# Input projection of a hybrid encoder step: six of seven column groups computed as block pairs with seven products each

## The chip, the cores and the metric

The kernel runs on one NeuronCore of a Trainium2 chip. TensorE (PE) multiplies; VectorE (DVE), ScalarE (ACT) and GpSimd (POOL) do elementwise work; SyncE (SP) issues most DMAs. Each engine runs its own list of instructions strictly in order and waits on semaphores. The metric is the device time of one execution in microseconds. Before the change it is 3000.38 us, the median of three runs (2999.57 to 3002.46).

## The reference, cut to what matters

```
h = rmsnorm(x, norm1_w) * (1 + sc1) + sh1                 # x: 2048 prompt rows, and 32 sample rows
mq, mk, mv, mo, mi, mf, sq, sk, sv = split_proj(h @ p['w_in'])   # 7 groups of 512 columns, 8 gate columns
y_a = rmsnorm(mlstm(mq, mk, mv, mi, mf)) * sigmoid(mo)
q_b, k_rows = rmsnorm(sq per head of 64), rmsnorm(sk per head of 64)
y_b = rmsnorm(stick_breaking(q_b, k_rows, sv))
x = x + g1 * (concat(y_a, y_b) @ p['w_out'])
x = x + g2 * conv_ffn(rmsnorm(x) * (1 + sc2) + sh2)
```

Only `h @ w_in` is touched: 1024 inputs, 7 x 512 + 8 outputs. The sample rows have their own state and modulation but the same weights. In the kernel the groups are numbered 0 mq, 1 mk, 2 mv, 3 sv, 4 mo, 5 sq, 6 sk, and it takes them in the order 0, 1, 2, 3, 5, 6, 4.

## The kernel before, in words

Three phases follow each other, each a block of instruction lists for all five engines with a barrier between: `front` (modulation, first norm, projection, gates), `attention`, and `mlstm_output_ffn`. Only `front` changes, and two scratch tensors in DRAM are added.

Products in fp32 precision are made from three passes in a rounded format: each operand is split into a high part (a rounded copy, by ACT) and a low part (the rest, by DVE or POOL), and high x high, low x high and high x low are summed in PSUM. One tile of 128 tokens by 512 columns by 1024 inputs is so 8 x 3 = 24 matmuls of 512 columns. The sample rows are tile 16; their high and low rows stand beside each other in one tile, so it takes 16 matmuls, and the two partial results are joined afterwards.

`front` has two stretches that matter here.

The prologue is group 0. It also makes `h`. For each of the 17 token tiles: SP loads x (`load_x`, L260); ACT squares and sums it and takes the root (`spread`, L331 and L333); DVE scales it (`scale_rows`, L459); PE transposes it (`turn_x`, L734); ACT and DVE apply scale and shift (`shift`, L352 and L464); ACT rounds it to the high part (L326); POOL makes the low part (`low`, L645); PE multiplies (`project`, L767); ACT moves the result from PSUM to a staging tile (`take`, L368); SP stores it (`store`, L277). There are three x buffers, four PSUM banks for results, and two for transposed x. The order is written out by hand: on ACT, item t is `take(t)`, `shift(t + 2)`, `spread(t + 4)`; on SP, `load_x(t + 3)` stands before `store(t)`, so that `load_x(t + 4)` stands behind `store(t)`; on PE, `project(t)` and then `turn_x(t + 2)`. The eight gate columns follow in one piece (`gates`, L783 and L785).

Groups 1 to 6 then run from SBUF alone: `h` stays there in high and low parts, and the next group's weights come in beneath the running one. In groups 5 and 6 DVE norms each tile per head (L560 to L571), PE transposes it (`turn`, L812), and the high and low parts go to DRAM for the attention (`store_turned`, L672 and L673). Group 4, with no norm, is last.

The later FFN phase already uses products of the new kind: its down projection (L3058) multiplies in units of seven products of 12 matmuls of 512 columns, and its sample rows (`sample_down`, L3029) in plain fp32.

Of the kernel before, what the change touches and what calls it, by code (L numbers as in the profile page):

```python
# [119 lines left out]
def front(k, c, gc, dec, firstK, firstQ):  # L120

    nc, d = k.nc, k.d
    NG, NN = 7, 2
    ORDER = (0, 1, 2, 3, 5, 6, 4)
    G0 = ORDER.index(5)
    FIRST = G0 * NT
    NQ = NG * KD
    NR, NW, NS, NB, NX = 2, 12, 3, 4, 3
    AHEAD = NW - KD
# [3 lines left out]
    END = (NG * NT - 1) % NS  # L133
    spans = [(n * W5, W5) for n in range(SEQ // W5)] + [(SEQ, P)]
    thirds = ((0, 172), (172, 342), (342, W5))

# [8 lines left out]
    raw_in = [k.sem(f"w_raw_loaded{n}") for n in range(2 * NR)]  # L145
    w_low_dve = k.sem("w_low_by_dve")
    w_high, w_low, w_used, summed, taken = k.sems("w_high", "w_low", "w_used", "projected", "psum_taken")
# [5 lines left out]
    sample_copied, sample_joined = k.sems("sample_copied", "sample_joined")  # L153
    wg_high, wg_low, gates_summed, gates_taken, pad_stored = k.sems(
        "wg_high", "wg_low", "gates_summed", "gates_taken", "pad_stored")
    gates_stored = [k.sem(f"gates_stored{n}") for n in range(3)]
# [6 lines left out]
        "rows_stored", "initial_ready", "last_kept", "norm_weights_loaded")  # L163
    with ExitStack() as s:
        with ExitStack() as early:
            h_plain = [sbuf(nc, early, f"h1_plain{n}", [P, KD, TOK]) for n in range(2)]
            xs = sbuf(nc, early, "px", [P, NX + 1, D])
        hH = sbuf(nc, s, "h1H", [P, KD, TOK], F32R)
        hL = sbuf(nc, s, "h1L", [P, KD, TOK], F32R)
        late = sbuf(nc, s, "plate", [P, NW - KD, 2, W5], F32R)  # L170
# [4 lines left out]
        nst = sbuf(nc, s, "pnst", [P, 2, 3, SH])  # L175
        nw = sbuf(nc, s, "pnw", [P, 2, SD])
# [18 lines left out]
        ada = h_plain[1][:, :, 0:4 * W5]  # L195
        bias, rows = h_plain[0][0:2, 0, 0:4 * W5], h_plain[0][0:2, 1, 0:4 * W5]
# [4 lines left out]
        h_raw = lambda t: h_plain[1][:, :, tok(t)]  # L201
        qH = lambda m: turnbuf[:, m % 2].rearrange("p (j e) -> p j e", e=P)
        qL = turnbuf[:, 2].rearrange("p (j e) -> p j e", e=P)
        sq, pT = R[:, 0:2], R[:, 2].rearrange("p (j e) -> p j e", e=P)
        g_out = lambda n, w: turnbuf[0:8, n % 3, 0:w].bitcast(F32)
# [9 lines left out]
        def normed(n):  # L215
            return FIRST <= n < FIRST + NN * NT

# [4 lines left out]
        def raw_slot(q):  # L222

            if q < 2 * KD:
                return q % NR, q // NR
# [3059 lines left out]
```

## Time and profile before

| | us |
|---|---|
| median of 3 runs | 3000.38 |
| the profiled execution | 3003.76 |
| its span, first to last instruction | 3002.1 |
| prologue (first `project` to last gate matmul) | 41.3 to 162.3 |
| groups 1 to 6 | 162.3 to 724.0 |
| first matmul of the attention | 728.3 |
| mean granted TensorE clock | 0.985 |

The span is what lies between the first and the last instruction of the profiled execution; the execution is 1.7 us longer. PE is busy 2890.5 us of the span, but matmuls overlap each other in these records, so that the distance between starts, not the busy time of one, is what a matmul costs.

### The profile page before, as it was taken

The page shows a single profiled execution, that of the slowest core. Times are in us where ns is not written, and L with a number is a line of the kernel's source. Part 1 is how long each engine was busy: PE and PEld are TensorE (multiplying, and loading weights), DVE is VectorE, ACT ScalarE, POOL GpSimd, SP SyncE. Part 2 cuts the span into 40 slices and gives each one's busy share as a digit, 9 for nine tenths or more (in the row PEclk, how much of TensorE's full clock was granted, in tenths as well). Part 3 has the DMA queues.
Part 4 walks back from the last instruction along what each step waited for, and adds up shares of the span by engine and source line. Part 5 has one row for each costly group of instructions (what it writes and reads, how often), then busy time and mean ns, then how long its engine had stood idle before and what let it go on. Part 6 is the DMA issues. An engine that isn't in the chain of part 4 may idle for free.

```text
span 3002.1 us, 48951 instructions
## 1 busy us (share of the span) xinstructions
PE 2890.5 (96%) x17179; PEld 2509.2 (84%) x17179; DVE 1949.0 (65%) x3087; ACT 1267.6 (42%) x2540; POOL 561.5 (19%) x585
## 2 busy tenths in 40 slices
PE   7999999999999999999998999999999898999998
PEld 5878888887777888798887999999999897777776
DVE  2300016732998999796668777777877777777765
ACT  4611112223777888554555333333432234333332
POOL 3310003312666776320110000000000000000000
PEclk9999999999999999999999999999999999999999
DMA  6322214543522232596564444444667777555565
GB/s 219 113 79 74 73 67 154 158 138 103 148 58 59 59 80 60 193 348 197 189 213 160 152 152 152 151 151 151 207 214 247 251 241 243 180 197 182 185 211 167
DMA packets 348223, 478.51 MB, mean 159 GB/s; under 512 B 69298, under 2 KB 222072, under 8 KB 345366
## 3 DMA queue, kind: packets, MB, share of 16 engines
q1 hardware_dynamic: 331240, 423.82, 44.6%
q0 software_dynamic: 15488, 52.52, 5.2%
q8 instruction: 94, 1.54, 0.2%
q14 instruction: 69, 0.57, 0.1%
q10 hardware_dynamic: 1332, 0.06, 0.0%
HBM read 297.49 MB, written 178.82 MB: 159 GB/s over the span
## 4 chain that ended last, share of the span: by engine, by line
PE 45%; DVE 6%; DMA 5%; issue 1%; ACT 1%; SPq 1%; DVEq 0%; ACTq 0%
PE facc L2928 24%; PE facc L3058 6%; PE eacc L2907 6%; PE dacc L3058 4%; DMA y_out<-dres 1%; PE mpT L3081 1%; DMA fsums<-sums_d 1%; PE mpm L3090 1%; DVE fV L2439 1%; PE mpS L3100 1%; PE eyT L2890 1%; PE mpT L3131 0%; PE mpN L3116 0%; PE exT L2920 0%; DVE fV L2435 0%
## 5 line engine op out<-in xcount | busy, mean ns | idle before, releaser
L2928 PE MATMUL facc<-fright,fsums 128*128 128x416 f32 x2112 | 420.7, 355 | 18.8 <-DMA fsums<-sums_d 9.4
L767 PE MATMUL pacc<-pring,h1H 128*128 128x512 f32 x1360 | 431.0, 394 | 3.8 <-ACT h1H L326 3.8
L2928 PEld LDWEIGHTS facc<-fright,fsums 128*128 128x128 f32 x2112 | 400.3, 191 | 25.9 <-issue 19.5
L1123 DVE TENSOR_TENSOR_SCAN aC<-aB,aC,a 128x512 f32<-128x512 f32 (+3 forms) x326 | 362.8, 1113 | 12.1 <-ACT aB L1079 1.1
L1183 POOL TENSOR_TENSOR aS<-aS,aC 128x512 f32<-128x512 f32 (+3 forms) x326 | 334.5, 1034 | 152.6 <-DVE aC L1123 146.0
L767 PEld LDWEIGHTS pacc<-pring,h1H 128*128 128x128 f32 x1360 | 256.2, 189 | 56.5 <-ACT h1H L326 3.9
L2928 PE MATMUL facc<-fright,fwH 128*128 128x416 f32 x1056 | 290.1, 356 | 12.0 <-DVE fU L2423 9.6
L767 PE MATMUL pacc<-pring,h1L 128*128 128x512 f32 x640 | 248.1, 389 | 0.0
L2928 PEld LDWEIGHTS facc<-fright,fwH 128*128 128x128 f32 x1056 | 199.4, 190 | 18.0 <-issue 12.1
L1203 PE MATMUL a_z<-ak,aq 128*128 128x512 f32 (+2 forms) x616 | 199.4, 405 | 0.5 <-DMA ak<-qk_T 0.5
L368 ACT ACTIVATE pstage<-pacc 128x512 f32<-128x512 f32 x112 | 66.5, 594 | 308.1 <-PE pacc L767 308.0
L1079 ACT ACTIVATE aB<-a_z 128x512 f32<-128x512 f32 (+3 forms) x326 | 180.6, 554 | 34.7 <-PE a_z L1203 18.7
L1229 PE MATMUL a_x<-ident,aS 128*128 128x128 f32 x1106 | 182.0, 281 | 10.4 <-ACT aA L1088 8.3
L2383 DVE TENSOR_TENSOR fwL<-fraw,fwH 128x1024 fp32r<-128x1024 f32 x86 | 93.4, 1087 | 151.4 <-ACT fwH L1994 151.4
L2928 PE MATMUL facc<-fh,fwH 128*128 128x416 f32 x704 | 189.9, 351 | 0.0
L1994 ACT ACTIVATE fU<-facc 128x416 f32<-128x416 f32 x132 | 67.3, 513 | 287.1 <-PE facc L2928 287.1
L2928 PE MATMUL facc<-fright,fwL 128*128 128x416 f32 x528 | 186.7, 354 | 0.0
L1084 ACT ACTIVATE aS<-a_z 128x512 f32<-128x512 f32 (+3 forms) x326 | 182.8, 561 | 0.0
L767 PE MATMUL pacc<-plate,h1H 128*128 128x512 f32 x544 | 177.8, 392 | 0.0
L1229 PEld LDWEIGHTS a_x<-ident,aS 128*128 128x128 f32 x1106 | 123.4, 140 | 53.8 <-issue 31.1
L1248 PEld LDWEIGHTS a_out<-aA,av 128*64 128x64 f32 x2176 | 122.7, 136 | 40.5 <-issue 30.7
L1248 PE MATMUL a_out<-aA,av 128*64 128x128 f32 x2176 | 154.3, 280 | 0.0
(388 smaller groups left out, 5627.9 us busy)
## 6 DMA issues: line engine op xcount, KB each, us to landing
sums_d<-fsums SPq DMA_DIRECT2D x88, 512.0 KB, 2.9
fsums<-sums_d SPq DMA_DIRECT2D x88, 512.0 KB, 4.6
fraw<-w_up SPq DMA_DIRECT2D x66, 512.0 KB, 4.0
proj_out<-pstage SPq DMA_DIRECT2D x119, 256.0 KB, 2.0
dres<-x_d SPq DMA_DIRECT2D x92, 256.0 KB, 3.4
qk_T<-pturn POOLq DMA_DIRECT2D x68, 256.0 KB, 3.1
mwa<-w_ada SPq DMA_DIRECT2D x16, 1024.0 KB, 6.3
dpart<-act_d SPq DMA_DIRECT2D x32, 512.0 KB, 3.8
```

The costliest lines, as they stand in the source:

```text
L767: op = mm_(acc[:, n % NB], h[:, kk, tok(t)], weight(q, w), start=(j == 0), stop=(j == len(order) - 1))
L1079: nc.scalar.activation(part(B, RB, n), part(Z, NZ, n), ACT.Sigmoid, scale=-1.0).then_inc(pass_ready, 1)
L1084: nc.scalar.activation(part(S, RS, n), part(Z, NZ, n), ACT.Sigmoid).then_inc(stop_ready, 1)
L1123: v.tensor_tensor_scan(buf[:, a:b][:, ::-1], part(B, RB, n)[:, ::-1], nought[:, 0:width(n)], buf[:, b:b + 1], ALU.mult, ALU.add).then_inc( ...
L1183: nc.gpsimd.tensor_tensor(at, at, buf[:, a + 1:b + 1], ALU.mult).then_inc(w_ready, 1)
L1203: mm = nc.tensor.matmul(to, q[:, i * P:(i + 1) * P], keys[:, span], start=(half == 0), stop=(half == 1), skip_group_check=True)
L1229: mm = nc.tensor.transpose(X[:, n % NX, j * P:(j + 1) * P], src[:, j * P:(j + 1) * P], c["ident"][:])
L1248: mm = nc.tensor.matmul(O[e * SD:(e + 1) * SD, u % 2, at:at + P], V[:, h % 2, b], weight[:, j * P:(j + 1) * P], start=lead, stop=(g == 0 a ...
L2383: v.tensor_tensor(upL[:, j, cols], raw[:, j, cols], upH[:, j, cols].bitcast(F32), ALU.subtract).then_inc(w_low[j], 1)
L2907: mm = nc.tensor.matmul(acc[:, 1 - i.u, cols], a[:, i.u, kk], w[:, kk, cols], start=(kk == 0 and n == 0), stop=(kk == KD - 1 and n == len( ...
L2928: mm = nc.tensor.matmul(bank, a[:, kk], b[:, kk], start=(begins and kk == 0 and m == 0), stop=(kk == count - 1 and m == 2), skip_group_che ...
L3058: mm = nc.tensor.matmul(banks[name], a[:, i], b, start=(name in ("P1", "P5", "P4") and i == 0 and m == 0), stop=(i == len(WINDOW[w]) - 1 a ...
```

## The change

Groups are taken in the pairs (1, 4), (5, 3) and (6, 2), tokens in pairs of tiles. Per pair of tiles and pair of groups, `h` is a 2 x 2 matrix of blocks (two tiles; even and odd 128-row pieces of the inputs: A11, A12, A21, A22) and the weights are one too (inputs; two groups: B11, B12, B21, B22). The four output tiles come from seven products of 12 matmuls each, with sums S1 to S4 of `h` blocks and T1 to T4 of weight blocks (the Strassen-Winograd scheme). That is a unit: 24 units (8 per pair), each of 84 matmuls.

Group 0 stays as it was, but the prologue now does more. `h` in fp32 goes to DRAM (`h1_d`, a DMA issued by ACT in `shift`), and the units load it from there, 512 KB for one tile. The T blocks of the first pair are made by DVE from rows that SP loads (`load_first_rows`, `t_sum`), and rounded by ACT (`t_high`); those of the other two pairs are made during the first eight units from w_in, stored to DRAM (`w1_sums`) and loaded at the change of pairs (`load_event`, `event_sum`, `store_event`, `load_cell`). The gate columns are made within the prologue, after every fourth tile.

The sample rows of the six groups are multiplied in plain fp32, with 32-column stationary tiles that write four different 32-partition parts of a bank (`sample_product`, 12 times 8 matmuls of 256 columns). The norms of groups 5 and 6 move to units 8 to 23, so that the last thing `front` does is now a normed tile. Per unit DVE makes 4 sums, 7 low parts and 3 output sums, ACT 7 high parts and 5 PSUM moves.

The main lines of the diff:

```diff
 # ACT, shift(t)
                 act.wait_ge(dve_part, t + 1)
-                copy(hH[:, :, tok(t)], h_raw(t)).then_inc(h_high, 1)
+                if t < NPT:
+                    at_least(act, h_low, t - 1)
+                    act.dma_start(d["h1_d"][t], h_raw(t)).then_inc(h_stored[t % 2], 16)
+                copy(hH[:, t], h_raw(t)).then_inc(h_high, 1)
...
 # ACT, the prologue's loop
             for t in range(NT):
-                if t == last - 1:
-                    for q in range(KD, NW):
-                        split(q)
-                take(t)
                 if t + 2 < NT:
                     shift(t + 2)
+                if t == last - 1:
+                    left_high_of("A11", 0)
...
+                take(t)
                 if t + 4 < NT:
                     spread(t + 4)
+                if t in (5, 7, 9, 11):
+                    t_high((5, 7, 9, 11).index(t))
+                if t == 13:
+                    cell_high_of(0, "B11")
...
 # SP, the prologue's loop
                 if t + NX < NT:
                     load_x(t + NX)
...
                 store(t)
+                if t % 4 == 0 and t > 0:
+                    store_gates(t // 4 - 1)
+                if t in (0, 5, 7, 9):
+                    load_first_rows((0, 5, 7, 9).index(t))
+                if t == 12:
+                    load_cell(0, "B11")
+                    load_cell(0, "B21")
...
 # PE
-            for t in range(NT):
-                project(t)
+            project(0)
+            turn_x(2)
+            for t in range(1, NT):
                 if t + 2 < NT:
                     turn_x(t + 2)
-            gates()
-            for g in range(1, NG):
-                for t in range(NT):
-                    project(g * NT + t)
...
+                project(t)
+                if t % 4 == 3:
+                    gates(t // 4)
+            gates(GATES - 1)
+            for w in range(UNITS):
+                unit(w)
...
+            def unit(w):
+                for name in PRODUCTS:          # P1, P5, P4, P6, P2, P7, P3
...
+                    for i in range(NK):
+                        for m, (a, b) in enumerate(((0, 0), (0, 1), (1, 0))):
+                            op = mm_(banks[name], lefts[one][:, a, i], cell(other, b)[:, i],
...
+                    if name == "P5" and w > FIRST:
+                        turn(norm_tile(w - 1, 0))
+                    if name == "P4":
...
+                        if 0 < w < len(EVENTS):
+                            sample_product(w)
+                    if name == "P6" and w > FIRST:
+                        turn(norm_tile(w - 1, 1))
...
+            def load_event(v):
...
+                elif v <= SUMMED:
+                    sp.wait_ge(event_stored, 16 * v)
```

ACT, prologue, one item before: it begins with the move of a result out of PSUM (L368); L352 and L326 are scale, shift and high part two tiles ahead, L331 and L333 square and root four tiles ahead.

```order
L368 ACTIVATE pstage<-pacc 128x512
L352 ACTIVATE h1_plain1<-pR,mod,A1 128x128 x4
L326 ACTIVATE h1H<-h1_plain1 128x8x128
L331 ACTIVATE px,pst<-px 128x1024
L333 ACTIVATE pst<-pst,eps 128x1
```

The same place on ACT after the change, item 7 and the beginning of item 8: L543 is scale and shift, L550 the new DMA, `pstage<-pacc` the move, L530 and L532 square and root, `pT` the new high parts.

```order
L543 ACTIVATE h1_plain1<-pR,mod,A1 128x128 x4
L550 DMA h1_d<-h1_plain1 128x1024
L525 ACTIVATE h1H<-h1_plain1 128x1024
L525 ACTIVATE pstage<-pacc 128x512
L530 ACTIVATE px,pst<-px 128x1024
L532 ACTIVATE pst<-pst,eps 128x1
L525 ACTIVATE pT0<-pT0_plain 128x2x512
L525 ACTIVATE pT1<-pT1_plain 128x2x512
L543 ACTIVATE h1_plain1<-pR,mod,A1 128x128 x4
L550 DMA h1_d<-h1_plain1 128x1024
L525 ACTIVATE h1H<-h1_plain1 128x1024
L525 ACTIVATE pstage<-pacc 128x512
```

The move out of PSUM stood ahead of scale, shift and high part and now stands behind them, and a DMA issue came between.

SP, prologue, items 5 and 6 after the change, with what each waits for: `px` is a tile of x, `proj_out` the store of a result, `praw` and `pturn` the rows of the first pair's weights.

```order
L356 DMA px<-x_all 128x1024 [waits x_turned_35]
L365 DMA proj_out<-pstage 128x512 [waits psum_taken_47]
L376 DMA praw<-w_in 128x512 [waits w_sums_104]
L376 DMA praw<-w_in 128x512
L376 DMA pturn<-w_in 128x512 x2
L356 DMA px<-x_all 128x1024 [waits x_turned_35]
L365 DMA proj_out<-pstage 128x512 [waits psum_taken_47]
```

Before the change loads and stores alternate here with nothing between them; the load of x still stands behind the store that waits for ACT's move.

DVE at the end of the first pair (units 7 and 8) after the change: L915 are low parts of `h` blocks, L882 low parts of whole weight blocks, L877 weight sums, L925 and L920 output sums.

```order
L882 TENSOR_TENSOR pT<-pT_plain,pT 128x4x512 [waits w_block_high_105]
L925 TENSOR_TENSOR pout<-pE,pacc 128x512 [waits out_stored31_134,bank_e_taken_123,products_119]
L907 TENSOR_TENSOR pS_plain<-ppart,pS_plain 128x512 [waits h_sums_116,products_119]
L915 TENSOR_TENSOR pS<-pS_plain,pS 128x512 [waits h_sums_116,h_left_high_117]
L915 TENSOR_TENSOR pS<-pS_plain,pS 128x512 [waits h_left_high_117]
L882 TENSOR_TENSOR pT<-pT_plain,pT 128x4x512 [waits w_block_high_105]
L882 TENSOR_TENSOR pB<-pB_plain,pB 128x4x512 [waits w_block_high_105]
L915 TENSOR_TENSOR pA<-ppart,pA 128x512 [waits h_left_high_117]
L882 TENSOR_TENSOR pT<-pT_plain,pT 128x4x512 [waits w_block_high_105]
```

In the kernel before, low parts of weights were spread one 128x512 piece at a time over DVE and POOL; here seven pieces of 128x4x512 stand in DVE's list within little more than one unit.

## Rows read from the trace of the kernel before

**Rows 1.** Windows by stage: busy time and count per engine, clock, DMA share, GB/s.
```profile
0.00:41.30 41.30, 19.40 (x224) 9.91 (x224) 9.50 (x28) 13.17 (x23) 14.69 (x32) 0.87 0.90 315
41.30:162.30 121.00, 120.96 (x599) 95.55 (x600) 38.52 (x98) 74.84 (x151) 50.76 (x28) 0.99 0.34 112
162.30:724.00 561.70, 561.70 (x2551) 464.26 (x2548) 153.96 (x264) 112.94 (x217) 83.61 (x98) 1.00 0.31 101
724.00:728.30 4.30, 0.01 (x1) 0.00 (x0) 0.68 (x1) 1.23 (x2) 0.00 (x0) 0.85 0.16 61
```
**Rows 2.** Timeline of ACT, one item of the prologue: start us, us, line.
```profile
125.82 0.58 ACT L368 ACTIVATE pstage<-pacc 128x512 f32<-128x512 f32 x1
126.30 1.49 ACT L352 ACTIVATE h_plain<-pR,mod,A 128x128 f32<-128x128 f32 x4
127.82 1.06 ACT L326 ACTIVATE h1H<-h_plain 128x1024 fp32r<-128x1024 f32 x1
130.65 1.06 ACT L331 ACTIVATE px<-px 128x1024 f32<-128x1024 f32 x1 [1.77 <-DMA px<-x_all]
131.83 0.29 ACT L333 ACTIVATE pst<-pst,eps 128x1 f32<-128x1 f32 x1
132.03 0.58 ACT L368 ACTIVATE pstage<-pacc 128x512 f32<-128x512 f32 x1
```
**Rows 3.** Line L368 in the prologue, and x's loads there: durations, first and last start.
```profile
L368 ACT ACTIVATE pstage<-pacc x16: 576/578/598, 48.5 to 147.4; 128x512 f32<-128x512 f32 x16
...
L260 SPq DMA_DIRECT2D px<-x_all x13: 431/433/1344, 49.5 to 126.8; - x13
...
DMA to landing us min/median/max: 3.8/3.9/4.6
```
**Rows 4.** Line L368 in group 1, and the matmuls around the phase's end.
```profile
L368 ACT ACTIVATE pstage<-pacc x11: 597/597/597, 200.8 to 258.8; 128x512 f32<-128x512 f32 x11
...
721.81 2.20 PE L767 MATMUL pacc<-pring,h1H 128*128 128x512 f32 x9
728.36 0.66 PE L1203 MATMUL a_z<-afirst_k,afirst_q 128*128 128x128 f32 x2 [4.34 <-PEq L71]
```
**Rows 5.** Timeline of PE in the FFN's down projection.
```profile
2589.05 2.96 PE L3058 MATMUL facc<-dB,dA 128*128 128x512 f32 x12
...
2605.78 2.96 PE L3058 MATMUL dacc<-dB,dS 128*128 128x512 f32 x12
2608.67 1.07 PE L3029 MATMUL facc<-draw_rows,dsample_act 128*32 128x256 f32 x16
2609.67 2.37 PE L3058 MATMUL facc<-dB,dA 128*128 128x512 f32 x9
```
**Rows 6.** Window of the down projection, columns as in rows 1.
```profile
2570.00:2850.00 280.00, 280.00 (x1270) 222.33 (x1269) 219.07 (x338) 101.31 (x174) 0.00 (x0) 1.00 0.55 183
```
**Rows 7.** Timeline of DVE: a norm in group 5, then independent instructions in the FFN.
```profile
547.36 0.69 DVE L560 TENSOR_TENSOR pR<-pstage 128x512 f32<-128x512 f32 x1
548.08 0.69 DVE L562 TENSOR_REDUCE pnst<-pR 128x8 f32<-128x512 f32 x1
549.14 0.20 DVE L565 RECIPROCAL pnst<-pnst 128x8 f32<-128x8 f32 x1 [0.37 <-ACT pnst L378]
549.38 0.69 DVE L567 TENSOR_TENSOR pstage<-pstage,pnst 128x512 f32<-128x512 f32 x1
550.10 1.66 DVE L571 TENSOR_TENSOR pstage<-pstage,pnw 128x512 f32<-128x512 f32 x1
...
2608.24 1.28 DVE L2591 TENSOR_TENSOR dres<-dres,dacc 128x512 f32<-128x512 f32 x2
```
**Rows 8.** Groups of 128x1024 work on DVE and ACT, durations as in rows 3.
```profile
L2559 DVE TENSOR_TENSOR draw_rows<-draw_rows,dgate x14: 1210/1218/1220, 2569.8 to 2814.4; 128x1024 f32<-128x1024 f32 x14
...
L1994 ACT ACTIVATE fwH<-fraw 128x1024 fp32r<-128x1024 f32 x64 | 67.4, 1053 | 1.6 <-DMA fraw<-w_up 1.6
L1994 ACT ACTIVATE fwH<-fraw 128x512 fp32r<-128x512 f32 x21 | 13.1, 623 | 0.0
```
**Rows 9.** DMA issues: count, KB each, median us to landing.
```profile
sums_d<-fsums SPq DMA_DIRECT2D x88, 512.0 KB, 2.9
mwa<-w_ada SPq DMA_DIRECT2D x16, 1024.0 KB, 6.3
qk_T<-pturn POOLq DMA_DIRECT2D x68, 256.0 KB, 3.1
praw<-w_in SPq DMA_DIRECT2D x36, 256.0 KB, 2.8
```
**Rows 10.** Windows in which PE idles part of the time, columns as in rows 1.
```profile
20.00:30.00 10.00, 5.08 (x60) 1.64 (x54) 1.96 (x6) 2.52 (x4) 3.36 (x3) 0.83 1.04 384
1230.00:1240.00 10.00, 7.64 (x31) 6.44 (x31) 4.57 (x8) 4.93 (x9) 0.00 (x0) 0.50 0.85 266
2890.00:3000.00 110.00, 93.98 (x413) 73.03 (x411) 66.38 (x119) 31.78 (x62) 0.00 (x0) 0.94 0.57 186
```

More of the change, by code:

```diff
@@ new lines, in bank_free, with product_of, user_of @@
+        def bank_free(eng, pos):
+            if pos < NB:
+                return
+            own = [n for n in range(GATES) if gate_position(n) == pos - NB]
+            if own:
+                eng.wait_ge(gates_taken, 2 * own[0] + 2)
+            else:
+                eng.wait_ge(taken, [t for t in range(NT) if position(t) == pos - NB][0] + 1)
+        def product_of(w, name):
+            return multiplied, 7 * w + PRODUCTS.index(name) + 1
+        def user_of(block_):
+            return next(name for name, sides in SIDES.items() if block_ in sides)
@@ new lines, in left, with left_index, half_place, h_blocks @@
+        def left(name):
+            return lefts[name][:, 0], lefts[name][:, 1], lefts_plain[name][:, 1]
+        def left_index(order, name, w):
+            return 7 * w + order.index(name) + 1
+        def half_place(w, e):
+            return part_first[e] if w == 0 else part[(2 * (w - 1) + 1 - e) % 3]
+        def h_blocks(w):
+            one, other = (half_place(w, e)[:].rearrange("p (k h) t -> p h k t", h=2) for e in range(2))
+            return {"A11": one[:, 0], "A12": one[:, 1], "A21": other[:, 0], "A22": other[:, 1]}
@@ new lines, in shift, with take, t_high @@
+                copy(hH[:, t], h_raw(t)).then_inc(h_high, 1)
+            def take(t):
+                n = position(t)
+                stage_free(act, n)
+                act.wait_ge(summed, t + 1)
+                copy(stage[:, n % NS], acc[:, n % NB]).then_inc(sample_copied if t == last else taken, 1)
+            def t_high(kp):
+                act.wait_ge(cell_sum, 4 * kp + 4)
+                for e in range(2):
+                    copy(t_cells[e][:, kp, :, 0], t_plain[e][:, kp, :, 1]).then_inc(cell_high, 1)
@@ L451, in _ @@
+            for m in range(NORMS - 2, NORMS):
+                take_turned(m)
         @block.vector
@@ L629, in _ @@
+            norm_end(UNITS - 1, 1)
+            for m in range(NORMS - 2, NORMS):
                 turned_low(m)
-            join_sample(NG - 1)
         @block.gpsimd
```

945 lines of the change are left out of this document (679 added, 266 removed).

## The prediction

> **What bounds the kernel now.** I read the windows by stage first. From 162.3 to 724.0 us, groups 1 to 6, PE is busy without a gap at full granted clock, with DVE at 27% and ACT at 20% [rows 1]: that stretch costs what its matmuls cost. Then there are 4.3 us in which nobody computes, the change of phase. In the prologue, 41.3 to 162.3 us, PE looks as busy, but the timeline of ACT says that two things bind it at once. One item of ACT begins at 125.82 and the next move out of PSUM at 132.03; in between ACT sits idle for 1.77 us until x has landed, and after that squares, takes the root and goes straight to the next move, with no wait for PE [rows 2]. So there is a ring: move out of PSUM, SP stores it, SP loads x four tiles ahead, ACT squares it, the next move. The scale, shift and high part (1.49 and 1.06 us) lie inside the wait for x and cost nothing. From 48.5 to 125.82 there are 12 such turns, 6.44 us each [rows 2, 3]. PE needs nearly the same, which is why the ring does not show.
>
> What a matmul costs I take from the distance of moves: from 200.8 to 258.8 us lie ten tiles of 24 matmuls and the sample's 16, 58.0 us for 256, so 0.2266 us each [rows 4].
>
> **The change part by part.**
>
> *Matmuls.* Before, 6 x 400 matmuls at 0.2266 are 543.8 us; with 34 turns the stretch is 561.7 us [rows 1], so a turn of four transposes costs 0.52 us. After, a product of 12 matmuls is priced by the down projection, which has this very form: from 2589.05 to the end of the one that starts at 2605.78 lie seven products, 19.53 us [rows 5] (I take 2.80 us for the last). 24 units are 468.7 us. The sample: 16 records, which are 8 fp32 matmuls, delay the next product from 2608.58 to 2609.67, so 1.09 us [rows 5], and 12 of them are 13.1 us. Thirty turns stay among the units, 15.6 us. Sum 497.4 against 561.7: PE's own saving is 64.3 us.
>
> *DVE in a unit.* Independent 128x512 instructions follow each other in 0.60 us, dependent ones in 0.72, and a norm takes two dependent ones, a wait of 0.37 and 0.20, and two more [rows 7]. Units 0 to 7: 4 sums, 7 low parts, 4 weight sums, 3 output sums, 18 x 0.60 = 11 us of 20.6. Units 8 to 23: 14 x 0.60, two norms of 3.4, two low parts of turned tiles, so 16.4, and ACT's 0.6 us hand-overs in between (each high part is waited for before its low part): following DVE and ACT from one S1 to the next I get 19.5 to 20.4 us, just below the 20.6 of PE. The down projection runs PE without a gap with DVE busy 219 of 280 us [rows 6]. I take nothing here; it can reach 1 us in each of 16 units.
>
> *Change of pairs, twice.* Seven weight blocks of 128x2048 must be split anew. From 512 and 1024 columns (0.69 and 1.22 us on DVE, 0.62 and 1.05 on ACT [rows 7, 8]) one costs 2.2 us on DVE and 1.9 on ACT, 15 us of DVE on top of a unit that leaves 4 to 9 us. They stand in DVE's list behind whatever waits there, five in the leaving unit, two (T3, B22) in the next. Written out from the first change: product 4 waits 2 us for T4, P6 3 us for T2, P7 5 us, because the copy that seeds its bank stands on ACT behind B22's high part: 10 us. In the second the norms stand in the same lists: 15 us. Both 25 us; low bound 12 (DVE's overload alone, with PE's slack in front), high 45.
>
> *Weight sums by way of DRAM, units 0 to 8.* A ring: sample product, two sums, A12's low part, two sums, store of 1 MB, load of 4 x 256 KB, the next sample product, behind which the rest of PE's list stands. PE, ACT and DVE make 9.9 us of it. 512 KB store in 2.9 us and 256 KB load in 2.8 [rows 9]; 1 MB each, with four issues of 0.4 us, I put at 4.4 and 4.3, so 18.6 of 20.6 us: hidden, and 3 us for small things. With the 6.3 us of a 1 MB load [rows 9] for each, 22.5 us, 8 times 1.9 = 15.
>
> *The prologue.* This is where I expect the time to go. In ACT's new list scale, shift, the DMA issue and the high part stand behind `spread` and ahead of the move. `spread(t + 4)` still waits for an x whose load SP issues behind the store that waits for the move of tile t. So the 2.54 us from the move's successor to the end of the high part leave the cover of the wait and enter the ring: 6.44 + 2.54 + 0.43 for the issue (the issue of the same 512 KB on SP [rows 3]) = 9.4 us per tile. Queued behind the waiting `spread` are `shift` of the next tile, on it the low part and `project` two tiles later: PE cannot run ahead. Into the same ring come: the four high parts of T, 4 x 2 x 1.02 = 8.2 us; four sets of first rows between store and x load on SP (1.6 us of issue and 1 MB ahead of x; 2.4 us each, 9.6), of which those of items 7 and 9 also wait for DVE's sums (2 us each, 4); two blocks of 1 MB ahead of the last x (5 us, counted below). The first move comes at 52.3 instead of 48.5, since `shift(2)` stands ahead of it. Twelve turns: 52.3 + 112.9 + 8.2 + 13.6 = 187.0, where before it was 125.8. From there before 36.5 us to the end of the gates; after, the last x (10.0), square, root, scaling and transposes (3.1), two tiles (10.9), the fourth gate piece (3.7), the sample tile and gates (4.1), 31.8 us, since the other gates lie in PE's idle time. Units begin at about 219, 56.5 us later than 162.3. Bounds: 43 without the delays by rows, 75 if x lands 1.5 us later in each turn.
>
> *The end.* Before, the attention starts 4.3 us after the last matmul. After, the last unit leaves two norms, their turns, low parts and POOL's stores (3.1 us to landing [rows 9]), which POOL waits for: P3 ends at 20.6 of the unit, the second norm at 25, the last low part at 27, the store at 31.5, then 2.2 us of change of phase: 13.1, so 8.8 more. Bounds 5 and 13. DMAs of the `h` tiles (1 MB per unit) land two units ahead: hidden.
>
> *Sum*: -64.3 + 25 + 3 + 56.5 + 8.8 = +29.0 us. On the profiled execution's 3003.8 that is 3032.8; it lay 3.4 above the median, so 3029 us against 3000.4.
>
> **A rule that speaks of the clock.** In windows in which PE idles part of the time the granted clock is 0.94 with 85% busy, 0.83 with 51%, and once 0.50, the lower of the two levels (1.2 of 2.4 GHz) [rows 10]. In my prologue PE idles about 3 us of 9.4. The Trainium skill (TensorE: Matmul & The Clock Gate, HAM oscillation — how this bites in real kernels) says that waits for DMAs between bursts of matmuls can throw the clock back each time; by it the prologue would be bound by PE at the lower clock. That is the fourth rival below, and by the rows, in which most such windows kept the higher clock, I give it little.
>
> **The rivals.**
> 1. *Faster: the ring stays at its old length.* If x lands so early that `spread` never waits, the prologue keeps PE's pace. For it: the unit savings are certain, and PE transposes one tile earlier. Against: x's load stands behind the store that waits for the move, whatever PE does, and landing took at least 3.8 us [rows 3]. The prologue would then grow by 3.8 + 8.2 - 4.7 = 7 us instead of 56.5: 3029 - 49 = 2980 us. It decides at a turn of 7.0 us: above that the saving is gone.
> 2. *DVE and ACT bind the normed units.* If hand-overs take a little more than I took, units 8 to 23 run at 21.8 us instead of 20.6 and both changes of pairs cost 20 us: +19 and +15, so 3063 us. For it: my own count leaves 0.2 to 1.1 us per unit. Against: the down projection holds full pace at 78% DVE [rows 6].
> 3. *The DRAM ring of the weight sums binds*: +12 us on the forecast, 3041; inside its range.
> 4. *The clock falls in the prologue.* At 1.2 GHz a tile takes PE 2 x (5.44 + 0.8) = 12.5 us, 3.1 more than the ring, 12 times: 3066 us.
>
> **How the numbers follow.** Forecast with rival 3: 0.62, own range 3006 to 3058 (prologue at 43 with changes at 15 gives 3006; upper bounds of changes and weight sums with a mid prologue give 3058). Rival 1: 0.14. Rival 2: 0.16. Rival 4: 0.08. Range 2995 to 3063: it leaves out most of rival 1 and the far halves of 2 and 4. A measurement of this kernel tells a change above about 0.2%, 6 us, from none. Slower by more than that: rivals 2 and 4 and nearly all of the forecast, 0.80. Within: 0.06, a forecast with all terms low or a weakened rival 1. Faster: 0.14.
>
> **What would show it.** Right: in the prologue ACT's moves lie about 9.4 us apart, each item with an idle wait for x of about 4 us, PE idle about a third, POOL's low parts waited for by PE; the first product near 219 us; 24 units of 20.6 us but for two of 30 to 36; the attention's first matmul near 757 us. Wrong: moves 6.4 us apart in the prologue (rival 1), distances of units of 8 to 23 near 22 us with PE released by DVE's low parts (rival 2), a granted clock near 0.5 before 219 us (rival 4), PE waiting in the sample products for w_in's rows in units 1 to 8 (rival 3). If the seven products cost other than 19.5 us per unit, the first term is wrong.

## The result, and the profile after

The changed kernel takes 3086.12 us (median of 4 runs, 3072.95 to 3092.1), the kernel before 3001.42 (4 runs, 2999.57 to 3002.74): ratio 1.0277, interval 1.0243 to 1.031. Forecast were 3029 us and a range up to 3063. The direction was right; the loss is 85 us instead of 29. The profiled execution of the changed kernel took 3072.95 us, the fastest of the four; its span is 3071.0 us. The two profiled executions differ by 69 us: the attention's first matmul comes 84 us later (812.45 against 728.3), and the rest of the program, whose code is the same in both, takes 15 us less. What follows explains the 84 us; the 15 us are taken up at the end of the account of the prediction. In experiments 5 and 8 one execution each fell into a slower state (4733 and 6558 us), and the times given there leave it out.

The windows of the changed kernel by stage. Columns: window, its length, busy time (instructions) of PE, weight load, DVE, ACT, POOL, then granted clock, DMA share, GB/s. The stages are the prologue, units 0 to 7, unit 8, units 9 to 15, unit 16, units 17 to 23, and the change of phase:

```profile
41.30:225.90 184.60, 138.32 (x600) 107.13 (x600) 70.08 (x130) 81.59 (x154) 40.68 (x18) 0.85 0.41 146
225.90:406.30 180.40, 167.01 (x809) 130.64 (x809) 104.07 (x185) 78.33 (x131) 7.24 (x14) 0.97 0.60 213
406.30:451.70 45.40, 24.42 (x101) 18.09 (x102) 29.02 (x33) 19.28 (x25) 0.00 (x0) 0.77 0.57 204
451.70:602.70 151.00, 144.63 (x693) 116.45 (x692) 109.12 (x178) 62.64 (x116) 19.48 (x26) 1.00 0.55 178
602.70:646.70 44.00, 26.70 (x94) 20.30 (x94) 32.71 (x38) 19.51 (x24) 4.49 (x6) 0.81 0.52 180
646.70:795.70 149.00, 141.61 (x645) 115.05 (x643) 107.08 (x178) 54.82 (x107) 20.89 (x28) 1.00 0.48 150
795.70:812.45 16.75, 1.70 (x9) 1.12 (x9) 4.83 (x9) 1.42 (x4) 3.02 (x6) 0.63 0.33 110
```

Against [rows 1]: PE was busy without a gap from 162.3 to 724.0 us. Now it lacks 46 us of 185 in the prologue, 21 of 45 in unit 8 and 17 of 44 in unit 16. The second view is PE's waits from 40 to 830 us (total, times, longest):

```profile
PE pR L1212 <- DVE px L760: 44.1, 10, 10.5
PE pR L1306 <- DVE psst L958: 24.5, 2, 16.2
PE pacc L1292 <- DVE pturn L951: 23.9, 13, 7.7
PE a_z L1735 <- PEq L71: 11.3, 1, 11.3
PE pR L1335 <- issue: 10.4, 5, 3.6
PE pacc L1335 <- DVE pT L882: 4.4, 1, 4.4
...
PE pR L1306 <- DMA pw_rows<-w_in: 1.6, 4, 0.6
```

L1212 transposes x, and waits for its scaling: that is the prologue's ring. L1306 is the sample product, and it waits 24.5 us in only two places for the squares of the sample rows (L958): nothing in the prediction stands for it. L1292 turns the q and k tiles. All five waits put down to "issue" (10.4 us) lie in units 8 and 16. The last row is the ring of the weight sums through DRAM: hidden. "PEq" is the change of phase.

The third view is the timeline of ACT from the end of one item to the end of the next, to be held against [rows 2]. The move is `pstage<-pacc`, L530 squares x, L543 scales and shifts, L550 issues the store of the tile, L525 copies high parts:

```profile
125.93 0.58 ACT L525 ACTIVATE pstage<-pacc 128x512 f32<-128x512 f32 x1
138.08 1.06 ACT L530 ACTIVATE px<-px 128x1024 f32<-128x1024 f32 x1 [11.57 <-DMA px<-x_all]
139.04 0.19 ACT L530 ACTIVATION_READ_ACCUMULATOR px<-px 128x1 f32 x1
139.26 0.29 ACT L532 ACTIVATE pst<-pst,eps 128x1 f32<-128x1 f32 x1
139.46 1.99 ACT L525 ACTIVATE pT<-pT_plain 128x1024 fp32r<-128x1024 f32 x2
141.35 1.48 ACT L543 ACTIVATE h_plain<-pR,mod,A 128x128 f32<-128x128 f32 x4
142.86 0.33 ACTq L550 DMA_DIRECT2D h_d<-h_plain  x1
143.24 1.06 ACT L525 ACTIVATE h1H<-h_plain 128x1024 fp32r<-128x1024 f32 x1 [0.40 <-ACT h_plain L543]
144.20 0.58 ACT L525 ACTIVATE pstage<-pacc 128x512 f32<-128x512 f32 x1
```

and SP's queue of the same item:

```profile
126.54 0.34 SPq L365 DMA_DIRECT2D proj_out<-pstage  x1
131.19 0.80 SPq L376 DMA_DIRECT2D praw<-w_in  x2
132.03 0.92 SPq L376 DMA_DIRECT2D pturn<-w_in  x2
133.00 0.43 SPq L356 DMA_DIRECT2D px<-x_all  x1
```

Everything of the ring is in these rows: the move (125.93), its store (126.54), the first rows, which wait until 131.19 for DVE's sums, x behind them (133.00), landed at 138.1, the square, T's high parts, scale, shift, issue and high part ahead of the move (144.20). That item takes 18.3 us. Items without rows take 8.9 to 9.3 us, as forecast (9.4). Those with rows take 12.3, 14.7, 18.3 and 16.3 us, where I had 12 to 16. Of two more, the one of 10.9 us holds the last high parts of T (1.99 us) and an ordinary wait for x (4.2 us), and the one of 15.3 us waits 10.5 us for an x behind the 1 MB blocks. The first product starts at 225.9 us, forecast near 219, before 162.3.

PE in units 4, 8 and 16. L1335 are the unit's products, twelve matmuls each:

```profile
327.66 1.93 PE L1306 MATMUL pR<-pw_rows,h_plain 128*32 128x256 f32 x16 [8.25 <-DVE psst L958]
...
417.04 4.57 PE L1335 MATMUL pR<-pT,pA 128*128 128x512 f32 x12 [3.64 <-issue]
437.82 1.93 PE L1306 MATMUL pR<-pw_rows,h_plain 128*32 128x256 f32 x16 [16.21 <-DVE psst L958]
...
623.42 5.46 PE L1335 MATMUL pacc<-pT,pS 128*128 128x512 f32 x12 [4.41 <-DVE pT L882]
636.57 1.09 PE L1292 MATMUL pacc<-ident,pout 128*128 128x128 f32 x4 [7.69 <-DVE pturn L951]
```

and DVE shortly before the row at 437.82:

```profile
433.99 2.29 DVE L882 TENSOR_TENSOR pB<-pB_plain,pB 128x2048 fp32r<-128x2048 f32 x1 [3.04 <-ACT pB L525]
436.20 0.69 DVE L915 TENSOR_TENSOR pA<-ppart,pA 128x512 fp32r<-128x512 f32 x1
436.80 0.42 DVE L956 TENSOR_TENSOR pR<-psample_y 64x256 f32<-64x256 f32 x1
437.26 0.42 DVE L958 TENSOR_REDUCE psst<-pR 64x4 f32<-64x256 f32 x1
```

The squares of a sample batch and their sums are 0.84 us of work (0.42 and 0.42). In unit 8 they stand in DVE's list behind the low part of B22 and the left block's low part, and the sample product of the same unit, in PE's list ahead of four products, may not reuse the bank before they are done. Where the profile says "issue" at 417.04, the cause can be read beside it: DVE's low part of T4, 414.65 to 416.94.

### The profile page after: what moved, and what is told of

Its sections match the earlier page's. It is cut to its first block, busy times and chain, and to the rows that moved or that the text cites. A ratio compares the mean times of both kernels' runs of the same rounds, so it can differ in the third digit from the quotient of the medians.

```text
span 3071.0 us, 49825 instructions
## 1 busy us (share of the span) xinstructions
PE 2852.6 (93%) x16979; PEld 2458.9 (80%) x16979; DVE 2211.3 (72%) x3468; ACT 1395.4 (45%) x2727; POOL 523.0 (17%) x555
## 4 chain that ended last, share of the span: by engine, by line
PE 44%; DVE 6%; DMA 4%; issue 1%; ACT 1%; SPq 1%; DVEq 0%; ACTq 0%
PE facc L3460 23%; PE facc L3590 6%; PE eacc L3439 6%; PE dacc L3590 4%; DMA y_out<-dres 1%; PE mpT L3613 1%; DMA fsums<-sums_d 1%; PE mpm L3622 1%; DVE fV L2971 1%; PE eyT L3422 0%; PE mpS L3632 0%; DVE fV L2967 0%; PE mpN L3648 0%; DVE fV L2976 0%; PE exT L3452 0%
## 5 line engine op out<-in xcount | busy, mean ns | idle before, releaser
L3460 PE MATMUL facc<-fright,fsums 128*128 128x416 f32 x2112 | 420.0, 355 | 16.3 <-ACT facc L2526 6.9
L3460 PEld LDWEIGHTS facc<-fright,fsums 128*128 128x128 f32 x2112 | 399.4, 190 | 23.5 <-issue 15.3
L1780 PEld LDWEIGHTS a_out<-aA,av 128*64 128x64 f32 x2176 | 122.6, 136 | 40.6 <-issue 30.8
L1335 PE MATMUL pacc<-pT,pS 128*128 128x512 f32 x576 | 145.6, 403 | 7.7 <-DVE pT L882 4.4
L2526 ACT ACTIVATE dS<-dS_plain 128x512 fp32r<-128x512 f32 (+1 forms) x96 | 57.3, 597 | 187.1 <-DVE dS_plain L3044 62.9
L1335 PE MATMUL pR<-pB,pA 128*128 128x512 f32 x576 | 141.4, 395 | 0.8 <-issue 0.6
L1335 PEld LDWEIGHTS pacc<-pT,pS 128*128 128x128 f32 x576 | 110.2, 194 | 38.4 <-issue 12.4
L525 ACT ACTIVATE pS<-pS_plain 128x512 fp32r<-128x512 f32 x96 | 60.7, 632 | 161.2 <-DVE pS_plain L899 61.9
```

What stands on the lines that cost most here:

```text
L1335: op = mm_(banks[name], lefts[one][:, a, i], cell(other, b)[:, i], start=(name in ("P1", "P5", "P4") and i == 0 and m == 0), stop=(i == NK ...
L1780: mm = nc.tensor.matmul(O[e * SD:(e + 1) * SD, u % 2, at:at + P], V[:, h % 2, b], weight[:, j * P:(j + 1) * P], start=lead, stop=(g == 0 a ...
L2526: copy = lambda to, at: nc.scalar.activation(to, at, ACT.Copy)
L3460: mm = nc.tensor.matmul(bank, a[:, kk], b[:, kk], start=(begins and kk == 0 and m == 0), stop=(kk == count - 1 and m == 2), skip_group_che ...
```

## The experiments

All ratios are against the kernel before, measured beside each run. In the code, `...` stands for lines left out. Where a profile is named, it is that of one execution and need not be one at the median.

**1. x one tile ahead** (changed kernel).

```diff
+            load_x(NX)
             for t in range(NT):
-                if t + NX < NT:
-                    load_x(t + NX)
+                if t + NX + 1 < NT:
+                    load_x(t + NX + 1)
```

> The changed kernel, but SP issues the load of x one tile earlier: ahead of the store of the tile before, no longer behind it. Theory (a ring of move, store, load of x, square, with the shift and high part inside it, and the first rows ahead of x): x no longer hangs on the store, so the ring is open, items fall from 9.8 to 16 us to PE's 6.3 to 6.6, the first product starts near 175 us instead of 226, and the time is 3086 - 50 = 3036 us. Rival A (the lowered TensorE clock or ACT's own list sets the pace, the loads are only late with it): first product at 215 or later, 3075 or more. Rival B (the DMA traffic of the first rows itself delays x): four items of 14 us stay, first product near 205, 3065.

Measured: 3041.33 us, ratio 1.0132 (1.0115 to 1.0149): 45 us less by one place in SP's queue. The first product starts at 184.2 us, most items take 6.3 to 7.6 us (one 10.0), but items 7, 9 and 11, in which ACT copies high parts of T, still 12. The ring is shown, and both rivals (3075 or more, 3065) are refuted; what stays in these items is the second wait, for DVE's sums (16.0 us in three waits of ACT), taken up in experiment 6. The lowered clock (0.85 in the prologue after, above) was its consequence: with the same matmuls, the clock from 50 to 150 us is 0.97, where the changed kernel's profile has 0.86.

**2. Move first** (changed kernel).

```diff
+                if t < last - 1:
+                    take(t)
                 if t + 2 < NT:
                     shift(t + 2)
...
-                take(t)
+                if t >= last - 1:
+                    take(t)
```

> The changed kernel, but ACT moves the finished tile out of PSUM ahead of scale, shift, issue and high part of the tile two later, as the kernel before does (tiles 0 to 14). Theory (ring): 1.48 + 0.37 + 0.40 + 1.06 us less what overlaps, about 2.9 us, leave the ring 12 times: first product near 226 - 35 = 191 us, items without rows 6.9 us, items with rows still 11 to 13; 3086 - 35 = 3051 us. Rival A (lowered clock sets the pace): under 8 us gained, 3078 or more. Rival B (low parts on POOL then come late for the matmuls, since the high part is issued later): PE waits for POOL, half is lost again, 3068.

Measured: 3078.67 us, ratio 1.0272 (1.0246 to 1.0298): the theory's 3051 was wrong, and so is rival B, since PE waits only 0.3 us for POOL there. The time is near that of rival A (3078 or more), but its reason does not hold: five of the eight moves without rows came 7.0 to 7.6 us apart instead of 9.1 (the ring's part, as expected) at the same granted clock (0.86 from 50 to 150 us in both). Those with rows took 11.4, 15.8, 19.8 and 20.0 us. SP in that run:

```profile
120.81 0.34 SPq L365 DMA_DIRECT2D proj_out<-pstage  x1
129.97 0.80 SPq L376 DMA_DIRECT2D praw<-w_in  x2
...
131.77 0.43 SPq L356 DMA_DIRECT2D px<-x_all  x1
```

The store left earlier, but the rows behind it wait 9 us for DVE's sums of the set before, and x's load behind them. SP's waits for these sums are 22.0 us in three places, against 6.4 us in two in the changed kernel: what the move gave, this wait mostly took back. That the sums' date hangs on the transposes and shifts, and so does not move with the move, is read from the lists and not tested alone. The prediction had 2 us for this wait, in two of the four sets.

**3. The kernel before with shift first.**

```diff
-                take(t)
                 if t + 2 < NT:
                     shift(t + 2)
+                take(t)
```

> The kernel BEFORE, with one edit: ACT's shift and high part of tile t+2 stand ahead of the move of tile t, as in the changed kernel; nothing else. Theory (ring): 2.54 us enter the ring 12 times, an item takes 9.0 us instead of 6.44, the prologue ends 30 us later: 3001 + 30 = 3031 us. Rival (PE or its clock sets the pace, ACT's order is free): 3001 to 3005 us.

Measured: 3029.31 us, ratio 1.0097 (1.0068 to 1.0125), as the ring says. ACT in it:

```profile
113.97 0.58 ACT L368 ACTIVATE pstage<-pacc 128x512 f32<-128x512 f32 x1
118.76 1.06 ACT L331 ACTIVATE px<-px 128x1024 f32<-128x1024 f32 x1 [4.21 <-DMA px<-x_all]
119.72 0.19 ACT L331 ACTIVATION_READ_ACCUMULATOR px<-px 128x1 f32 x1
119.94 0.29 ACT L333 ACTIVATE pst<-pst,eps 128x1 f32<-128x1 f32 x1
120.14 1.49 ACT L352 ACTIVATE h_plain<-pR,mod,A 128x128 f32<-128x128 f32 x4
121.67 1.06 ACT L326 ACTIVATE h1H<-h_plain 128x1024 fp32r<-128x1024 f32 x1
122.63 0.58 ACT L368 ACTIVATE pstage<-pacc 128x512 f32<-128x512 f32 x1
```

8.7 us from move to move, and ACT is idle for 4.2 of them, until x has landed. PE's waits in that run name someone else, which is the trap:

```profile
PE pacc L767 <- POOL h1L L645: 19.9, 13, 2.3
```

**4. Shift first and x one tile ahead** (kernel before): the edits of 3 and 1 together, so that the two readings of that row come apart.

```diff
+            load_x(NX)
...
-                take(t)
                 if t + 2 < NT:
                     shift(t + 2)
+                take(t)
```

> The kernel BEFORE with two edits: ACT's shift and high part ahead of the move (alone: 3029 us), and x loaded one tile earlier. Theory (the order costs only because x hangs on the store, a ring): with the ring open the order of ACT's list is free, items fall from 8.75 back to 6.3 us, 3000 us. Rival (in the run with the shift first PE waited 19.9 us for POOL's low parts: ACT's order delays the low parts in themselves): stays within 5 us of 3029.

Measured: 3000.0 us, ratio 1.0001 (0.999 to 1.0012), moves 6.3 to 6.4 us apart. The order in ACT's list costs nothing once x does not hang on the store; POOL was only the last link of a late chain, and the rival, which needed a time within 5 us of 3029, is refuted.

**5. x one tile ahead alone** (kernel before; SP's queue as in experiment 1).

```diff
+            load_x(NX)
...
+                    load_x(t + NX + 1)
```

> The kernel BEFORE with one edit: x loaded one tile earlier. Theory (ring of 6.44 us beside PE's own 6.24 per tile): 12 times 0.2 us, 2999 us, 2 us less. Rival (PE alone set the pace before): 3001, no difference.

Measured: 2999.71 us, ratio 1.0 (0.999 to 1.0009): no difference that can be told. The moves lie 6.3 to 6.4 us apart in it, so before, PE was the bound and the ring lay exactly beside it, without a price.

**6. x one ahead, and the high parts of T one item later** (changed kernel).

```diff
-                if t in (5, 7, 9, 11):
-                    t_high((5, 7, 9, 11).index(t))
+                if t in (6, 8, 10, 12):
+                    t_high((6, 8, 10, 12).index(t))
```

> The kernel of the run with x one tile ahead (3041 us), and ACT's high parts of T stand one item later, so that ACT no longer waits 5.5 us in its list for DVE's sums of the first rows. Theory (what is left of the prologue's loss is this second wait, four times): the items of 12 us fall to about 8, DVE's own list of 12.5 to 15 us per two items now sets them; 12 to 16 us less, 3027 us. Rival (PE's matmuls and DVE's shifts wait for the same sums, wherever ACT's copy stands): under 3 us gained, 3039.

Measured: 3034.43 us, ratio 1.0116 (1.0101 to 1.013), 7 us less than experiment 1 by the medians (5 by the ratios), half of what was expected. The first product came at 174.9 instead of 184.2. Items of 11.3 to 12 us stayed, but each is now followed by one of 4.7 to 5.1.

**7. Sample rows taken and squared a unit earlier** (changed kernel).

```diff
-                if w in (4, 8, 12):
-                    take_sample(w // 4 - 1)
...
+                if w in (3, 7, 11):
+                    take_sample(w // 4)
...
+                if w in (3, 7):
+                    sample_squares(w // 4)
```

> The changed kernel, but the sample rows are taken from their bank and squared at the end of units 3, 7 and 11 instead of inside units 4, 8 and 12, ahead of the sample product that reuses the bank. Theory: the waits of 8.25 and 16.2 us of the sample products of units 4 and 8 go; unit 4 falls from 30.8 to 21.5, unit 8 from 45.4 to 32 to 38, since the seven new weight blocks of that unit remain: 3086 - 17 = 3069 us. Rival (DVE's and ACT's own work on the new weight blocks binds these units anyway; the wait for the sample only shows it): the products behind wait instead, under 5 us gained in all, 3082 or more.

Measured: 3068.62 us, ratio 1.0232 (1.0215 to 1.025), 17.5 us less. In its profile unit 4 fell from 30.8 to 23.9 us and unit 8 from 45.4 to 37.2; the profiled executions differ by 10.7 us up to the attention, since unit 5 took 4 us more. The wait was the cause and not a sign of DVE's load: 15 of its 24.5 us came back in the two units themselves, and the rival's 3082 or more did not come.

**8. A second bank for the transposes** (changed kernel).

```diff
+        pT = lambda m: (bank_s if second(m) else bank_t)...
...
-                at_least(pe, turn_low, m)
+                at_least(pe, turn_low, m if m < SECOND else m - 1)
```

> The changed kernel, but the transposed tiles with odd numbers from unit 13 on go to the sample rows' bank, which is free by then, so PE need not wait for the low part of the tile before. Theory (the single bank of the transposes stalls PE in every normed unit, a wait that the prediction did not price): the waits of 0.5 to 2.5 us in ten units go and the 7.7 us of unit 16 shrink to 3 or less: units 14 to 23 fall from 21.1 to about 20.2, 12 to 16 us less, 3072 us. Rival (DVE and ACT bind these units, the wait only shows it): the wait moves to the product behind it, under 3 us, 3084.

Measured: 3079.49 us, ratio 1.0257 (1.0238 to 1.0276): 7 us less than the changed kernel, which three runs and an interval that overlaps its 1.0243 to 1.031 do not tell from nothing. In the profile units 13, 14 and 16 fell to 20.0, 21.3 and 41.6 us (from 21.7, 22.3 and 44.0), but unit 15 rose to 24.6 (from 21.2); those from 649 us on kept 20.5 to 21.9, but for unit 22. From the first product of unit 8 to the last of unit 23 it is 387.5 us, against 386.5. PE's wait for the low part of a turned tile fell from 23.9 to 0.6 us, its waits for the copies by ACT that seed a bank rose from 3.3 to 9.8, those for DVE's normed tile from 1.1 to 7.6. One such unit of that run:

```profile
696.44 0.66 PE L1296 MATMUL pacc<-ident,pout 128*128 128x128 f32 x4
696.85 3.01 PE L1339 MATMUL pR<-pT,pA 128*128 128x512 f32 x12
700.27 2.98 PE L1339 MATMUL pacc<-pT,pS 128*128 128x512 f32 x12 [0.42 <-ACT pacc L527]
703.09 0.60 PE L1296 MATMUL pR<-ident,pout 128*128 128x128 f32 x4
```

The second turn (703.09) no longer waits, the product before it does. That the wait moves is what the rival said, and the 12 to 16 us of the theory did not come. The large wait for the turn (23.9 us in 13 pieces) was never worth 23.9 us.

**9. No new weight blocks** (changed kernel; loads, high and low parts of the new blocks are left out and PE does not wait for them, so that units 8 to 23 use the first pair's blocks and their outputs are other numbers).

```diff
-                coming = w // HALF + 1 if w % HALF == HALF - 1 and w + 1 < UNITS else None
+                coming = None
...
-                leaving = more and n % HALF == 0
-                arriving = w > 0 and w % HALF == 0
+                leaving = arriving = False
```

> The changed kernel without the changes of pairs: the seven weight blocks of the second and third pair are neither loaded nor split, units 8 to 23 multiply with the blocks of the first pair (so their outputs are other numbers). Theory: the splitting on DVE and ACT costs 16 us in unit 8 beside the wait for the sample, and 23 us in units 16 and 17 (21.1 us is a normed unit without it): 39 us less, 3047 us, unit 8 at about 29 with the wait of the sample product left at 8, unit 16 at 21. Rival (the prediction's 25 us were right, the rest is the wait for the sample): 3061 us.

Measured: 3041.21 us, ratio 1.0134 (1.0117 to 1.0151): 45 us less. In the profile unit 8 took 30.6 us (7.5 us of wait for the sample are left in it) and unit 16 took 21.2: 14.8 and 22.8 us less. So the two changes cost 38 us by the units of one execution, 45 by the medians, where the prediction had 10 + 15 and the rival of this run 3061 us. The 7 us between the two figures have no place in a trace: up to the attention the two profiles differ by 35.5 us. The edit takes away the loads, ACT's high parts and DVE's low parts together, so it does not say which of them is the price.

**10. Four edits together** (6 with 7 and 8).

```diff
+                    load_x(t + NX + 1)
...
+                if t in (6, 8, 10, 12):
...
+                if w in (3, 7, 11):
...
+        second = lambda m: m >= SECOND and m % 2 == 1
```

> The changed kernel with four edits together: x loaded one tile earlier, high parts of T one item later, sample rows taken and squared a unit earlier, second bank for the transposes. Theory: the gains add, since they lie in different stretches: 45 + 13 + 17 + 14 = 89 us off 3086: 2997 us, within 0.4% of the kernel before. Rival (part of each gain only moves a wait that DVE's work then takes over in units 4, 8 and 16): 3010 us or more.

Measured: 3016.65 us, ratio 1.0056 (1.0044 to 1.0068). The loss fell by 69.5 us where 89 were expected, and the rival's number, 3010 or more, came true. Of the 20 us that are missing, 7 are the second bank's and 6 experiment 6's, both over-estimated beforehand. Against the gains as they were measured one by one (45, 7, 17.5 and 7 us) 6 are missing, which these runs do not tell from scatter: units 4, 8 and 16 took 23.1, 37.4 and 40.7 us here and 23.9, 37.2 and 41.6 with their edit alone, so the rival's reason is not seen there.

**11. Rows behind x, and a buffer for the last low part** (on top of 10).

```diff
...
+                if t in (1, 6, 8, 10):
+                    load_first_rows((1, 6, 8, 10).index(t))
...
-                if t in (0, 5, 7, 9):
-                    load_first_rows((0, 5, 7, 9).index(t))
```

> The kernel of the run with four edits (3017 us) and two more: SP issues the first rows of w_in behind the next load of x, not ahead of it, and the last low part of the transposed tiles has a buffer of its own, so that DVE does not wait 4.9 us for the store before it. Theory: what is left of the prologue's loss are x loads that lie 1.8 us of issue and 1 MB behind the rows (ACT still waits 4 to 5 us for x once in two items): 5 to 8 us less there, 3 to 4 less at the end, 3006 us. Rival (the traffic itself delays x, whatever the order): only the end gains, 3013.

Measured: 3011.2 us, ratio 1.0035 (1.0023 to 1.0048). ACT no longer waits for x anywhere, but the first product starts at 176.8 us, no earlier than the 174.8 of experiment 10: the order of rows and x was not what was left, and only the end gained, as the rival said: 2.8 us (14.0 from the last product to the attention, from 16.8). The medians are 5 us apart, but the intervals overlap, and in both profiles the attention starts at 745.9 us.

**12. T3 and B22 split later** (on top of 11; ACT's list, and DVE's in the same way).

```diff
-                if arriving:
-                    cell_high_of(w // HALF, "T3")
                 if more:
                     left_high_of("S1", n)
                 take_e(w)
                 if arriving:
-                    cell_high_of(w // HALF, "B22")
+                    cell_high_of(w // HALF, "T3")
...
                 seed_c(w)
+                if arriving:
+                    cell_high_of(w // HALF, "B22")
```

> The kernel of the run with rows behind x, and in the first unit after each change of pairs the two last weight blocks (T3, B22) are split later: behind the copies and low parts that the earlier products wait for. Theory (of the 16 and 20 us that a change costs, a part is order: PE waits 5.7 and 3.6 us for the copy that seeds a bank, which stands behind these blocks in ACT's list): 6 to 9 us less, 2999 us. Rival (DVE's load is the price, the order only says where it shows): under 2 us, 3005.

Measured: 3008.13 us, ratio 1.0026 (1.0016 to 1.0037): 3 us less, between theory and rival, and its interval overlaps that of experiment 11 (1.0023 to 1.0048), so that it may be nothing. Units 8 and 16 went from 36.5 and 42.0 to 35.8 and 40.6. The order of the blocks is at most a small part. PE's waits there are now mostly for DVE's low parts of blocks (12.5 us in four waits), which speaks for DVE's work as the price; no run moved part of it to POOL, so this is argued and not shown. This is the best version of the change that was found, and it is still behind the kernel before: its first product starts 14 us later, its end is 9.7 us longer, and its 24 units take 551.5 us against 561.7. By the profiles its attention starts 13.4 us later, by the medians it loses 7.

## Why the prediction was wrong

Up to the attention's first matmul the forecast was 757 us; measured are 812.45, so 55 us more. They divide as follows, from the starts of the units in the trace (the forecast puts every unit at its mean, 497.4 / 24 = 20.7 us, and adds the 3, 10 and 15 us where they belong):

| Place | forecast us | measured us | more |
|---|---|---|---|
| first product | 219 | 225.9 | 7 |
| units 0 to 7, with the sums' ring | 168.8 | 180.4 | 11.6 |
| unit 8 | 30.7 | 45.4 | 14.7 |
| unit 16 | 35.7 | 44.0 | 8.3 |
| the 14 other units | 290.2 | 300.0 | 9.8 |
| last product to attention | 13.1 | 16.75 | 3.6 |

- *The step that failed is the pass over PE's list of a unit.* The prediction counted the sample product as 1.09 us of matmuls and followed its wait for w_in's rows only. It waits also for its bank, which the sample norm of the batch before holds, and in unit 8 that norm stands behind the new blocks in DVE's list. Two waits, 8.25 and 16.2 us; experiment 7 took them away and won 17.5 us. They are not all of the miss: without them the kernel took 3068.6 us, still 6 above the range. The other large part, 13 to 20 us, is the mis-sized changes of pairs, below.
- *The ring of the prologue was right.* Items without rows: 9.4 forecast, 8.9 to 9.3 measured; experiments 1, 3, 4 and 5 show the mechanism in both kernels, and what it costs alone (28 us, forecast 12 x 2.54 = 30). The twelve turns took 136.3 us (53.53 to 189.79), forecast 134.7. The 7 us more of the prologue are 1.2 before the first move, 1.6 in the turns and 4.3 behind them. That the turns come out so close is in part luck: items without rows were shorter than forecast, those with rows longer. The rows' wait for DVE's sums was put at 2 us twice and measured 4.3 in the item shown and 2.1 in item 9, and near 9 in experiment 2.
- *The changes of pairs* were mis-sized: 25 forecast (bounds 12 and 45), 38 to 45 by experiment 9. Experiment 12 shows that order is at most some 3 us of that. What PE waits for there, product by product, are DVE's low parts and ACT's copies, and the product behind each long wait runs at a lower clock; which of DVE's work, ACT's work and the loads it would pay to take away stays open.
- *PE's own saving* was under-estimated. A product takes 2.72 us where nothing waits, not 2.79 (the first two of unit 11):

```profile
495.60 2.88 PE L1335 MATMUL pR<-pB,pA 128*128 128x512 f32 x12
498.32 2.89 PE L1335 MATMUL pR<-pT,pS 128*128 128x512 f32 x12
```

Seven are 19.04 us, and a turn adds about 0.45, so a normed unit could take 19.9. The saving was 12 us larger than forecast; waits of ACT's seeds and DVE's low parts, 0.2 to 2.5 us each, ate it and more in units 9 to 23.
- *Normed units.* Rival 2 said 21.8 us, the forecast 20.6; the 14 without a change took 21.4 in the mean. I gave rival 2 a chance of 0.16; in the units it came true to two thirds of its height (21.4 of 21.8 us), and in the changes of pairs to the full (38 to 45 us, rival 2 said 40).
- *Rival 3* (the sums' ring): 1.6 us of waits. Refuted. *Rival 4* (the clock): the clock did fall, to 0.85 in the prologue, and eight transposes took 1.97 us instead of 1.03 in eight items, yet it did not set the pace: experiment 2 has items of 7.0 to 7.6 us at the same granted clock, and in experiment 1 the clock rose with the ring opened. *Rival 1*: refuted, and experiment 1 shows what it would have needed, x one place earlier in SP's queue.
- *The range.* The measured time lies 23 us above its upper end. Its bounds were bounds of size on waits that had been found. The sample's bank wait, 17.5 us, was in none of them, and both changes of pairs came out near their upper bound (38 to 45 of 45 us) at once with the end above its middle. The upper end of the forecast's own range is also added up too low: 3029 + (45 - 25) + (15 - 3) is 3061, not 3058.

What stays open. The stretch from the attention's first matmul to the end of the span took 2258.6 us in the changed kernel's profile and 2273.7 in that of before, though its code is the same. In the four profiles of kernels with the front of before it takes 2267.2 to 2273.7 us, in the ten with a changed front 2258.6 to 2267.3, in the mean 6 us less. So one part is scatter between single executions, and another seems to be a gain of some 6 us that the prediction did not have and for which no run here shows the cause. It fits experiment 12, which is 13.4 us behind at the attention's start and 7 by the medians. The median of the changed kernel lies 13 us above its profiled execution; the kernel of experiment 8, profiled at 3086.02 us, has 4 of them ahead of the attention and 9 behind its start.

## What to carry to other kernels

List, for every instruction of the bounding engine, all the semaphores it waits for, and for each the place of its setter in the other engine's list, before counting any work: two waits of 24.5 us together were here for 0.84 us of work each, in the wrong place. Where a load's issue stands behind a store in one queue, move the load one item ahead first; that alone gave back 45 of 85 us, and in the kernel before it made the order of ACT's list free (3029.31 to 3000.0 us). The length of a wait in the profile is no price: 24.5 us of waits for the sample were worth 17.5, 23.9 us for the turn were worth about 7, and perhaps nothing.

## What the runs showed of the hardware

DVE and POOL can slow each other when both work on SBUF. In the changed kernel's trace, a 128x512 subtraction on DVE takes 0.68 us, and 2.89 when POOL's low part runs beside it:

```profile
126.95 0.68 DVE L854 TENSOR_TENSOR pT_plain<-pturn,praw 128x512 f32<-128x512 f32 x1
127.55 2.89 DVE L856 TENSOR_TENSOR pT_plain<-pturn,pT_plain 128x512 f32<-128x512 f32 x1
```

```profile
127.34 2.55 POOL L1122 TENSOR_TENSOR h1L<-h_plain,h1H 128x1024 fp32r<-128x1024 f32 x1 [6.53 <-DMA h_d<-h_plain]
```

In experiment 1 two of POOL's low parts took 6.82 us together instead of 4.8; beside them two of DVE's low parts of T took 4.57 us instead of 2.35, and a subtraction 2.88 instead of 0.68. This was read, not tested by a run of its own. The Trainium skill (SBUF — State Buffer, SBUF: two separate sides) says that the two share a pair of ports as an exclusive lock, which, between an instruction of DVE with two inputs in SBUF and one of POOL that reads SBUF, the one that starts first holds for its whole length. By that rule DVE's subtraction would start at 129.89, when POOL ends, and with 0.6 us for one end at 130.5, an estimate; it ended at 130.44, so the rows agree.

A wait of PE costs more than its length. The same twelve matmuls take 2.88 us where no wait stands before them, 3.00 after a wait of 1.13 us, 4.56 after 3.41, and 5.46 after 4.41 (granted clock 0.77 and 0.81 in units 8 and 16). The length of the wait alone does not fix it: in experiment 12 they took 4.58 us after 4.43. In unit 16 that adds some 6 us to the waits, and a list of waits does not show it.
